# A weight ring of 14 slots of 1 MB in place of 12, in a four-layer transformer kernel on one core

## What is computed

```python
x = x + concat([mix, mem_out]) @ w_out                  # the mixer of the layer
x = x + hierarchical_moe(rms_norm(x, g), ...)

def hierarchical_moe(h, w_group, b_group, w_expert, b_expert, w_gate, w_up, w_down):
    g_prob = softmax(t @ w_group + b_group); g_idx = argmax(g_prob)      # one of 4 groups
    e_sel  = (t @ w_expert + b_expert) of that group
    top_w, top_i = top_k(softmax(e_sel), 2)                              # two experts of it
    gate = einsum('td,edf->tef', t, w_gate); up = einsum('td,edf->tef', t, w_up)
    act  = silu(gate) * up * combine[..., None]
    return einsum('tef,efd->td', act, w_down)
```

## Time and profile before

| | |
|---|---|
| median of 3 runs | 1532.49 us (1529.9 to 1535.6) |
| profiled execution, span | 1536.0 us, 23584 instructions (the page gives no other time of it) |
| TensorE busy | 1432.1 us (93%) |
| DVE, ACT, POOL busy | 737.2 (48%), 495.9 (32%), 102.6 us (7%) |
| HBM read | 465.42 MB; 305 GB/s over the span |

### The profile page before, as it was taken

One profiled execution on the slowest core, in us unless ns is written; L12 is line 12 of the kernel. 1 busy time (PEld: TensorE's weight loads), 2 busy tenths in 40 slices (PEclk: granted clock), 3 DMA queues, 4 the chain that ended last, 5 costly groups with the idle time before them and its releaser, 6 DMA issues. The chain is left out here.

```text
span 1536.0 us, 23584 instructions
## 1 busy us (share of the span) xinstructions
PE 1432.1 (93%) x9090; PEld 786.3 (51%) x9090; DVE 737.2 (48%) x1659; ACT 495.9 (32%) x996; POOL 102.6 (7%) x258
## 2 busy tenths in 40 slices
PE   7999999987899899998888998999899998989998
PEld 4585533322365644332227876788655336765432
DVE  1467432222255544222226755675585346668534
ACT  3231211111226412111116656565512116661211
POOL 0000011100000001110102000200001102000110
PEclk9999999999999999999999999999898999999999
DMA  8798799999963189999997462335169996437997
GB/s 358 313 365 334 294 381 417 421 420 422 426 266 145 59 336 386 398 422 420 421 424 302 165 225 77 110 143 227 42 230 422 420 425 248 174 156 301 422 420 299
DMA packets 63399, 469.78 MB, mean 306 GB/s; under 512 B 7809, under 2 KB 15921, under 8 KB 18738
## 3 DMA queue, kind: packets, MB, share of 16 engines
q1 hardware_dynamic: 63282, 468.22, 75.2%
HBM read 465.42 MB, written 2.76 MB: 305 GB/s over the span
## 5 line engine op out<-in xcount | busy, mean ns | idle before, releaser
L1671 PE MATMUL PS<-ring,catT 128*32 128x512 f32 x3072 | 348.0, 594 | 18.8 <-issue 16.4
L826 PE MATMUL PS<-w_split,h_split 128*128 128x512 f32 x1152 | 272.7, 396 | 6.0 <-DVE w_split L911 6.0
L826 PEld LDWEIGHTS PS<-w_split,h_split 128*128 128x128 f32 x1152 | 215.5, 190 | 56.9 <-DVE w_split L911 8.5
L1671 PEld LDWEIGHTS PS<-ring,catT 128*32 128x32 f32 x3072 | 96.4, 110 | 235.0 <-issue 234.8
L911 DVE TENSOR_TENSOR w_split<-ring,w_split 128x512 fp32r<-128x512 f32 x192 | 132.6, 705 | 69.3 <-ACT w_split L859 68.7
L1694 PE MATMUL PS<-ring,row_place 128*32 128x512 f32 x1232 | 142.3, 593 | 20.2 <-issue 20.1
L859 ACT CAST w_split<-ring 128x512 fp32r<-128x512 f32 x192 | 118.0, 619 | 106.7 <-PE PS L826 106.2
L1869 ACT ACTIVATE row_place<-PS 128x256 f32<-128x256 f32 x48 | 18.4, 384 | 367.7 <-PE PS L1671 367.7
L1694 PEld LDWEIGHTS PS<-ring,row_place 128*32 128x32 f32 x1232 | 41.4, 110 | 112.1 <-issue 112.1
L508 PE MATMUL PS<-ring,catT 128*128 128x512 f32 x224 | 96.7, 592 | 1.0 <-PEq L1022 1.0
L1564 POOL COPY catT<-xsT 128x256 f32 x176 | 63.3, 404 | 405.4 <-PE PS L1671 397.8
(11 more groups left out here) (445 smaller groups left out, 1869.2 us busy)
## 6 DMA issues: line engine op xcount, KB each, us to landing
ring<-in_moe SPq DMA_DIRECT2D x269, 1024.0 KB, 15.2
ring<-in_w_ada SPq DMA_DIRECT2D x16, 3072.0 KB, 12.2
ring<-in_a_w_in SPq DMA_DIRECT2D x23, 2048.0 KB, 14.4
ring<-in_b_w_in SPq DMA_DIRECT2D x8, 2048.0 KB, 20.1
first_down<-in_moe SPq DMA_DIRECT2D x8, 1024.0 KB, 8.5
ring<-in_a_w_out SPq DMA_DIRECT2D x2, 3072.0 KB, 18.3
ring<-in_b_w_out SPq DMA_DIRECT2D x2, 3072.0 KB, 13.9
ring<-in_w_mem_kv SPq DMA_DIRECT2D x2, 2048.0 KB, 11.5
```

What stands on the lines that cost most here:

```text
L826: last = nc.tensor.matmul(PS[:, 2 * (i % 2) + t, :], hs[:, hp, k, t * P:(t + 1) * P], wk[:, (KT * i + k) % splits, wp, :], start=k == 0 an ...
L1671: last = nc.tensor.matmul(PS[lanes, 4 + i % 2, :].rearrange("p (g f) -> p g f", g=2), xf[:, i % 2, k, lanes], gate_up_weights(2 * i + q % ...
```

## The change

`RING` becomes `14 * 2048` = 28672 values per partition in place of 24576: 14 slots of 1 MB. The 16 KB per partition for it come from three places: the scratch that dynamic transfers get is cut to 1024 bytes; the tile `zero` is 128 columns wide instead of 512, and the filler products take as moving operand one column of `ones_b`, repeated 512 times by a step of 0 (their weights stay the zeros, so the products are still 0); and `bias_row` is made only where there is a shift. So that no transfer is issued from GpSimd any more, the store and the column loads of `every_token` move to ScalarE's program: the first four columns ahead of the loop, the others behind the activation of each expert.

```diff
--- before.py
+++ after.py
@@ -27,7 +27,7 @@
 KT = D // P
 EPS = 1e-6
 NEG = -1e30
-RING = 4 * 6144
+RING = 14 * 2048
 LOADS = 16
 FF = 256
 PIECE = 2048
@@ -228,7 +228,7 @@
         mod_gain = sbuf(ctx, "again", [P, 2, 2, 8])
         not_before = sbuf(ctx, "not_before", [P, P], BF16)
         ones_b = sbuf(ctx, "ones_b", [P, P], BF16)
-        zero = sbuf(ctx, "zero", [P, BANK], BF16)
+        zero = sbuf(ctx, "zero", [P, P], BF16)
 
         r_loaded = sig("router_loaded")
         x_normed = catT[:].rearrange("p k t -> p (k t)")[:, 0:TT * D].rearrange("p (t d) -> p t d", t=TT)
@@ -378,7 +378,7 @@
         def keep_busy(bank, n):
 
             for _ in range(n):
-                nc.tensor.matmul(PS[:, bank, :], zero[:, 0:P], zero[:], start=True, stop=True)
+                nc.tensor.matmul(PS[:, bank, :], zero[:], ones_b[:, 0:1].to_broadcast([P, BANK]), start=True, stop=True)
 
         def norm_to_T(src, gain, shift, dst, keep=None, normed=False):
 
@@ -1381,7 +1381,7 @@
                 xn_split = [sbuf(st, "xn_split", [P, TT, D], F32R), xn_low_rows]
                 slot_of = sbuf(st, "slot_of", [P, NP])
                 picks = sbuf(st, "picks", [P, TT, E], BF16)
-                bias_row = sbuf(st, "bias_row", [P, C])
+                bias_row = sbuf(st, "bias_row", [P, C]) if shift is not None else None
                 lg = sbuf(st, "rl", [P, TT, C])
                 el = sbuf(st, "el", [P, TT, E])
                 w12 = sbuf(st, "rw", [P, 2, TT, E])
@@ -1543,13 +1543,6 @@
                     pool.wait_ge(*table_ready.at(1))
                     def every_token(pool):
 
-                        pool.wait_ge(*ct_sb.at(1))
-                        nc.gpsimd.dma_start(A["comb_dram"][0:E, :], combT).then_inc(c_stored.sem, 16)
-                        pool.wait_ge(*c_stored.at(16))
-                        for e in range(E):
-                            if e >= 4:
-                                pool.wait_ge(*up_taken.at(e - 3))
-                            nc.gpsimd.dma_start(cb[:, e % 4, :], A["comb_dram"][e:e + 1, :].to_broadcast([P, T])).then_inc(cb_loaded[e % 4].sem, 16)
                         nc.gpsimd.sem_inc(win_ready.sem, 2 * E + 4)
 
                     far_from_here("gpsimd", f"rows_{m}", block.end_bb, every_token)
@@ -1745,7 +1738,7 @@
                             last.then_inc(xt_ready.sem, 1)
                         for b in range(4):
                             pe.wait_ge(*xt_taken.at(4 + b + 1))
-                            nc.tensor.matmul(PS[:, b, :], zero[:, 0:P], zero[:], start=True, stop=False, skip_group_check=True)
+                            nc.tensor.matmul(PS[:, b, :], zero[:], ones_b[:, 0:1].to_broadcast([P, BANK]), start=True, stop=False, skip_group_check=True)
                         pe.wait_ge(*h_shifted.at(KT))
                         pe.wait_ge(*ct_sb.at(1))
                         gate_up_all(0)
@@ -1829,11 +1822,23 @@
                         take_ranks_and_weights(act)
                         act.wait_ge(*ct_ready.at(1))
                         nc.scalar.copy(combT, PS[0:E, 4, 0:T]).then_inc(ct_sb.sem, 1)
+
+                        def load_column(e):
+                            nc.scalar.dma_start(cb[:, e % 4, :], A["comb_dram"][e:e + 1, :].to_broadcast([P, T])).then_inc(cb_loaded[e % 4].sem, 16)
+
+                        act.wait_ge(*ct_sb.at(1))
+                        nc.scalar.dma_start(A["comb_dram"][0:E, :], combT).then_inc(c_stored.sem, 16)
+                        act.wait_ge(*c_stored.at(16))
+                        for e in range(4):
+                            load_column(e)
                         for e in range(E):
                             act.wait_ge(*gate_ready.at(e + 1))
                             if e >= 2:
                                 act.wait_ge(*hid_ready.at(e - 1))
                             nc.scalar.activation(sg[:, e % 2, :], PS[:, 4 + e % 2, :], ACT.Silu).then_inc(silu_ready.sem, 1)
+                            if e + 4 < E:
+                                act.wait_ge(*up_taken.at(e + 1))
+                                load_column(e + 4)
                         nc.scalar.sem_inc(y_high.sem, highs)
 
                     far_from_here("scalar", f"every_silu_{m}", f"rejoin_act_{m}", every_token)
@@ -3269,7 +3274,7 @@
     feeds["slot_no"] = np.arange(S2).astype(np.float32)
     feeds["desc"] = np.arange(32, 0, -1).astype(np.float32)
 
-    nc = bacc.Bacc("TRN2", target_bir_lowering=False, num_devices=1)
+    nc = bacc.Bacc("TRN2", target_bir_lowering=False, num_devices=1, dynamic_dma_scratch_size=1024)
     A = {"col_at": col_at}
     arrays = {}
     for name, v in feeds.items():
```

## The result

The changed kernel takes 1516.35 us (median of 4 runs, 1506.89 to 1523.2), the kernel before 1532.88 us beside it (4 runs). The ratio is 0.9877, 95% interval 0.9835 to 0.9918. The forecast was 1522.4: right in sign, too small in size. By the three runs' median that it started from, 1532.49, the ratio means about 1514, a gain of 19 us where 10.1 were expected, and just outside the range's lower end of 1516. Over all comparisons of this study the gap is 17.5 us: 63 runs of the kernel before have a mean of 1533.4, 28 runs with the 14-slot ring a mean of 1515.9.

The account below looks back on a forecast made before the run. The prediction took DMA to bound the later part of MoE 0 and 1 and TensorE the earlier. Part 1's 10.1 us, with 0 from the rest, taken from the median 1532.49 gave 1522.4 us; range 1516 to 1530, 8 in 10.

Parts of the forecast that it names:

- What bounds the kernel: MoE 0 and 1: TensorE-bound early at 11.94 us a pair of experts, DMA-bound late at 15.17 us.
- Part 1, MoE 0 and 1: Two more pieces loaded ahead of each of the two stages, 2.53 us a piece: 10.1 us gained.
- Part 1, MoE 2 and 3: These stages, with 8 pairs each, end before their stock of pieces does: gain 0.
- chunk 116: A 3 MB load in front of MoE 1, needing 113 used chunks instead of 114, goes out a block earlier.
- Part 2 and 3: Step-0 filler products, and the left-out bias row with the moved column loads: taken as 0 us.
- The bandwidth rule: Expert piece loads: at the skill's 358 GB/s a piece takes 2.93 us and four give 11.7; the measured rate was preferred.
- B: Rival: the extra stock is there in only one of MoE 0 and 1; gain 5 us, 1527.4; chance 0.13.
- C: Rival: no gain, MoE 0 and 1's late period being set by release-to-reload time; 1532.5; chance 0.05.
- D: Rival: step-0 fillers at each head take twice their interval, costing 20 us; 1542; chance 0.07.
- A: Rival: the clock at a stage's head changes, 2.7 us either way, up to 5.4 for two; within the forecast's 0.72.

Follow-up runs that it names:

- e2: The changed kernel with the ring put back to 12 slots, all else of the change kept: 1534.33 us, ratio 0.9994 to the kernel before.
- e7: The changed kernel with 13 slots in the ring instead of 14: 1529.36 us, ratio 0.9978 to the kernel before.
- e5: The changed kernel with 14 slots for the experts' 1 MB pieces only, other loads within the first 12: 1521.9 us, ratio 0.9927 to the kernel before.
- e6: The changed kernel with expert pieces wrapping after 12 slots, all other loads allowed 14: 1525.83 us, ratio 0.9964 to the kernel before.
- e3: The changed kernel with 14 slots, but fillers reading 512 different columns instead of one repeated: 1517.9 us, ratio 0.989 to the kernel before.

## Why the prediction was off, point by point

**What bounds the kernel.** Right for MoE 0 and 1: the plateaus, the split into a TensorE-bound and a DMA-bound part, "issue" as waits for pieces. The waits of both lines over the whole span fall with the slots for pieces: 37.5 us in e2, 33.3 in e7, 29.1 in e5, 26.2 in the changed kernel.

**Part 1, MoE 0 and 1.** The mechanism is right: 14 ahead, 77 after, first stall at 318.47 (forecast 319), 26.2 us of waits left (forecast 28), late period 14.91 us (forecast 15). The size was too small. The last landing moves by 207.7 - 202.3 = 5.4 us in MoE 0 and by 208.0 - 201.4 = 6.6 us in MoE 1, together 12.0 instead of 10.1. I had three readings of a piece and took the middle one, 2.53, from the period. The third, 2.58, from SyncE's restart to the stage's end, is the better one, because it is over that whole stretch that the pieces drop out: measured from the restart to the last landing a piece took 2.56 to 2.58 us in MoE 0 and 2.58 to 2.61 in MoE 1. That gives 5.1 and 5.2 us, 10.3 in all, and so explains only 0.2 of the missing 1.9 us. In MoE 1 the piece was also a little shorter with 14 slots (2.588 on average against 2.606), which over 76 pieces is 1.4 us more. It doesn't follow the slots: it took 2.605 with 13 and 2.584 with 10. Why, the runs don't say.

**Part 1, MoE 2 and 3.** This is the step that failed. "MoE 2 and 3 gain 0" rested on one window, 1480 to 1500 us, and that is MoE 3. I carried it over to MoE 2 without reading a row there. MoE 3 does stay the same (103.4 to 105.0 us in the profiles of either ring). But MoE 2 was at its DMA limit, hidden by a head that the clock had made 4 us longer, and e6 shows that 3.8 us were to be had with no more slots for its pieces than before. The bandwidth line of the earlier trace rows could not have told the two apart: it has 420 over MoE 2 and over MoE 3. The text had even noted such a load in front of MoE 1 (chunk 116) and drawn nothing from it for MoE 2.

**Part 2 and 3.** 0 and 0, as e2 and e3 show. The Trainium skill (SBUF — State Buffer, the note on cachelines) says that consecutive accesses to the same 16-byte line run at full bandwidth, and a step of 0 stays in one line; e2, with 12 fillers in 2.77 us, agrees.

**The bandwidth rule.** The windows after still show 420 to 423 GB/s. The Trainium skill (DMA: Bandwidth & Descriptors, section Bandwidth) has about 358 for loads from HBM, and by that a piece would be an estimated 2.93 us. The measured 2.56 to 2.61 us a piece contradict it. The same section limits the figure, which the prediction left out: it gives about 358 to each core when both cores of an HBM domain stream, and 425 for a 16 MB load with the other core idle. The 420 to 423 here, with one core at work, agree with that. That its 11.7 us for the four pieces lies near the measured 12.0 is chance.

**The sum.** 5.4 + 6.6 + 3.8 = 15.8 us by the stages, 14.0 by the runs at equal clock, 17.5 by the runs as they are; 10.1 was forecast. MoE 2, put at 0, is the largest term that was missing, and MoE 0 and 1 lacked 1.9. The 3.5 between 14.0 and 17.5 go with the clock, which the forecast had as a spread of both signs; whether the ring causes them is open.

**The rivals.** B (stock in one stage only) and C (no gain) are out: e5 shows both stages shorter, by 5 and 7 us. D is out by e2. A was there, but I gave it as a spread of both signs about heads, 2.7 us each. Heads do change sides (head 0 took 16.6 us in most profiles, 18.3 in one and 19.9 in two), and that evens out. What did not even out in the profiles is the dilated attention, 25 against 13 us at half clock, which I never looked at, since the change does nothing in it.

**The range.** It reached 6.4 us below the forecast. An honest bound on what MoE 2 had to give, and on the clock in a stage of 338 us with 25 us of half clock, would have put the low end near 1512.

## What to carry to other kernels

When a prefetch ring grows, list for every stage when its stock is complete and when its last load lands relative to its first use; a stage with next to no stalls may still be at its DMA limit, if something slow in front of it gave the loads their time. A sum of a stage and its head that stays constant while the parts change (124.4 to 124.6 us here) shows such a limit. And a claim about a stage needs a row from that stage.

## What the runs showed of the chip

- Runs of the same kernel spread over a mean granted clock of 0.974 to 0.989 (changed kernel), and 1.1 us of time goes with each 0.001. A single profile can thus be 9 us off its kernel's mean: the changed kernel's first took 1506.89 us, where 28 runs have 1515.9.
- At gaps of TensorE of 2.2 to 2.7 us in the dilated attention the granted clock fell to 0.50 for 3.4 to 10.2 us in nearly every profile. 30 fillers in all, 6.5 us of otherwise idle time at 0.216 each, brought 25 us at half clock down to 3 in the kernel before, and took 8.1 us off its time; in the changed kernel 13 came down to 4, and 5.9 us went.
- A moving operand that reads one bf16 column 512 times with a step of 0 passes as quickly as 512 different columns: 12 in a row take 2.77 us against 2.75, and e2 and before, e3 and the changed kernel beside it differ by less than 1 us.
- Loads of 1 MiB from one core's queue ran at 420 to 423 GB/s for whole windows of 20 us, beside a TensorE that was busy for all of 200 to 220 us.
